# Two PSUM banks for the projections of the local pairs, a bank of its own for their second value batch, another order on GpSimd, and the first local K projected a pair ahead

## The reference, cut to what matters

```python
def even_mixer(h, w_in, w_out, rpb):
    B, T, _ = h.shape
    proj = (h @ w_in).astype(jnp.float32)
    cuts = np.cumsum([W_A, W_A, W_A, W_B, W_B])
    qa, ka, va, qb, kb, vb = jnp.split(proj, cuts, axis=-1)
    ...
    ya = dilated_mixture_attention(heads(qa), heads(ka), heads(va))
    yb = neighborhood_attention(heads(qb), heads(kb), heads(vb), rpb)
    y = jnp.concatenate([ya, yb], axis=1).transpose(0, 2, 1, 3).reshape(B, T, W_A + W_B)
    return y.astype(h.dtype) @ w_out
```

## Time and profile before

| | |
|---|---|
| Runs of the kernel | 2565.6, 2570.64, 2570.91 us, median 2570.64 |
| The profiled execution | 2565.84 us, span 2563.9 us |
| TensorE busy | 2510.9 us, 98% of the span |
| VectorE, ScalarE, GpSimd busy | 1755.5, 1156.1, 413.8 us |
| Granted TensorE clock, mean | 0.993 |
| Pair 3 (with the projection of pair 4) | 247.1 to 309.3 us |
| Pairs 4, 5, 6 | 309.3 to 379.1, to 437.2, to 496.1 us |
| Pair 7 and the first items of the output projection | 496.1 to 545.9 us |

### The profile page before, as it was taken

How to read it: one execution, slowest core, us unless ns; L and a number is a source line. 1 busy time by engine, 2 the same in 40 slices (tenths; PEclk the granted TensorE clock), 3 DMA queues, 4 the chain that set the end, 5 groups by cost and what they waited for, 6 DMA issues and landing times.

```text
span 2563.9 us, 34993 instructions
## 1 busy us (share of the span) xinstructions
PE 2510.9 (98%) x12931; PEld 2068.9 (81%) x12931; DVE 1755.5 (68%) x2647; ACT 1156.1 (45%) x2016; POOL 413.8 (16%) x320
## 2 busy tenths in 40 slices
PE   9999989899999999999999999999999999999998
PEld 7888767778888888888888888888888888888887
DVE  6555545565788888765577777777657878877655
ACT  6555534443433333444455555456434333334444
POOL 1000022310133333200010000000001332332001
PEclk9999999999999999999999999999999999999999
DMA  3222134642344444776411111112233444447754
GB/s 128 61 61 73 38 86 104 157 166 103 133 168 160 162 152 158 281 251 203 147 45 49 44 46 49 49 49 79 107 110 117 167 177 156 145 171 257 238 192 146
DMA packets 189171, 332.38 MB, mean 130 GB/s; under 512 B 59728, under 2 KB 67792, under 8 KB 180816
## 3 DMA queue, kind: packets, MB, share of 16 engines
q1 hardware_dynamic: 154208, 320.62, 36.9%
q10 hardware_dynamic: 34800, 9.60, 1.7%
HBM read 238.24 MB, written 91.91 MB: 129 GB/s over the span
## 4 chain that ended last, share of the span: by engine, by line
PE 92%; DVE 2%; issue 2%; ACT 2%; DMA 1%; SPq 1%; POOL 1%; ACTq 0%; POOLq 0%; DVEq 0%
PE PS L2362 20%; PE PS L2280 18%; PE PS L2281 18%; PE PS L2282 18%; PE PS L2523 4%; PE PS L2455 4%; PE PS L2479 3%; PE PS L2471 1%; PE PS L2429 1%; PE PS L2500 1%; PE PS L2376 1%; PE PS L2504 1%; DVE WS L1585 1%; PE PS L2288 0%; PE PS L2419 0%
## 5 line engine op out<-in xcount | busy, mean ns | idle before, releaser
L2362 PE MATMUL PS<-HH,WS 128*128 128x512 f32 x1536 | 519.8, 405 | 24.5 <-DVE FS L1709 14.1
L2362 PEld LDWEIGHTS PS<-HH,WS 128*128 128x128 f32 x1536 | 287.5, 190 | 84.7 <-DVE FS L1709 15.0
L2362 PE MATMUL PS<-HL,WS 128*128 128x512 f32 x768 | 303.3, 395 | 0.0
L2081 DVE TENSOR_TENSOR SPLIT<-RAWI,SPLIT 128x1024 fp32r<-128x1024 f32 x154 | 195.4, 1271 | 149.2 <-ACT SPLIT L1434 148.7
L1434 ACT ACTIVATE SPLIT<-RAWI 128x1024 fp32r<-128x1024 f32 x154 | 162.9, 1060 | 205.3 <-PE PS L2282 155.8
L2280 PE MATMUL PS<-TH,WS 128*128 128x512 f32 x640 | 249.0, 389 | 0.0
L2281 PE MATMUL PS<-TL,WS 128*128 128x512 f32 x640 | 249.0, 389 | 0.0
L2282 PE MATMUL PS<-TH,WS 128*128 128x512 f32 x640 | 249.0, 389 | 0.0
L2280 PE MATMUL PS<-SPLIT 128*128 128x512 f32 x616 | 240.2, 390 | 0.0
L2282 PE MATMUL PS<-SPLIT 128*128 128x512 f32 x616 | 239.7, 389 | 0.0
L2281 PE MATMUL PS<-SPLIT 128*128 128x512 f32 x616 | 239.7, 389 | 0.0
(11 more groups left out here) (274 smaller groups left out, 4967.0 us busy)
## 6 DMA issues: line engine op xcount, KB each, us to landing
WR<-wstrips SPq DMA_DIRECT2D x224, 256.0 KB, 2.7
RAWI<-ab_scratch SPq DMA_DIRECT2D x154, 256.0 KB, 4.0
ab_scratch<-SIL SPq DMA_DIRECT2D x132, 256.0 KB, 2.0
WD<-wdown SPq DMA_DIRECT2D x22, 1024.0 KB, 6.8
wd_scratch<-WD SPq DMA_DIRECT2D x22, 1024.0 KB, 3.9
RAWI<-wd_scratch SPq DMA_DIRECT2D x88, 256.0 KB, 3.2
UR<-wstrips SPq DMA_DIRECT2D x80, 256.0 KB, 3.1
RAWI<-wdown SPq DMA_DIRECT2D x66, 256.0 KB, 3.7
```

Source lines behind the costliest of these rows:

```text
L2081: e.tensor_tensor(SPLIT[m % 6][:, 1], RAWI[:, m % 4], f(SPLIT[m % 6][:, 0]), ALU.subtract).then_inc(S["ilo"], 1)
L2362: last = e.matmul(ps, wt, xt, start=g == 0, stop=g == 23)
```

## The change

It has six parts. (1) Scores of pairs 4 to 6 take banks 0 and 1 in every slot (`score_bank`); `qk(P, n)` waits for the exps of the slot just before, through the same semaphore. Pair 7 keeps its four score banks. (2) Bank 2 is then a second projection bank (`STRIPE_BANK`): parts 3, 5 and 1 of pairs 5 and 6 go there, parts 3 and 5 of pair 7, and part 1 of pair 4; their `fill` waits for the evacuation of the part before the last one. (3) Bank 3 takes the second value batch (`VALUE_BANK`); for pair 7 it is bank 7. (4) On GpSimd, `kq_low` of parts 2 and 3 stands ahead of `merge_start`, and of parts 4 and 5 ahead of `merge_rest`. On SyncE, `raw` of the second strip stands ahead of `merge_second`, and of the third ahead of `merge_store`. (5) The whole part k = 2 of pair 4 is made in pair 2's last slot, and each later part of pair 4 takes two whole slots of pair 3; the evacuations come a slot earlier, the two weight strips are split in slots 0 and 3 in place of 2 and 5, and `lo` of head 1 is put behind the evacuation of the next slot for n = 1, 3, 5 in place of 0, 2, 4. (6) `spread_rstd` in `classical` moves from ahead of the product k = 2 to the middle of it, 12 matmuls later.

```diff
-    FILLS_TURN = [([(1, 2, 16, 20)], [(1, 2, 20, 24)])]
-    FILLS_TURN += [([(1, k, a, a + 6 + u)], [(1, k, a + 6 + u, a + 12)]) for k in (3, 4, 5) for a, u in ((0, 3), (12, 0))]
-    FILLS_TURN += [([(1, 0, 0, 12)], [(1, 0, 12, 24)])]
+    FILLS_TURN = [([(1, k, a, a + 6 + u)], [(1, k, a + 6 + u, a + 12)])
+                  for k in (3, 4, 5, 0) for a, u in ((0, 3), (12, 0))]
...
-            return [parts[0], [(2, 2, 0, 16)]]
+            return [parts[0], [(2, 2, 0, 24)]]
...
-    START_TURN, START_B, MID_B = {1: 2, 3: 3, 5: 4, 7: 5}, {2: 2, 5: 4, 6: 5}, {3: 3, 7: 0}
+    START_TURN, START_B, MID_B = {0: 2, 2: 3, 4: 4, 6: 5}, {2: 2, 5: 4, 6: 5}, {3: 3, 7: 0}
...
-        return n == 4 if P < 3 else P == 3 and n in (0, 2, 4)
+        return n == 4 if P < 3 else P == 3 and n in (1, 3, 5)
...
-        return {**({1: (3, 0, 5)} if late(P) else {}), 2: (4, 1, 6), 5: (5, 0, 8)}
+        if P == 3:
+            return {0: (4, 1, 6), 3: (5, 0, 8)}
+        return {1: (3, 0, 5), 2: (4, 1, 6), 5: (5, 0, 8)}
...
+    def score_bank(P, n, m):
+        return m if 4 <= P < 7 else 2 * (n % 2) + m
+
+    def fill_bank(P, k):
+
+        if P in (5, 6) or P == 7 and k != 1 or P == 4 and k == 1:
+            return STRIPE_BANK if STRIPE_ORDER[k] % 2 else FILL_BANK
+        return FILL_BANK
+
+    def tv_bank(P, b):
+        return PV_BANK if kind_of(P) != "B" or b == 0 else FILL_BANK if P == 7 else VALUE_BANK
...
+    STRIPE_BANK, VALUE_BANK = 2, 3
...
                     merge_first(P - 4)
-                    merge_second(P - 4)
                 raw(w + ahead + 1, layer)
                 if 4 <= P < 7:
+                    merge_second(P - 4)
+                raw(w + ahead + 2, layer)
+                if 4 <= P < 7:
                     merge_store(P - 4)
-                raw(w + ahead + 2, layer)
...
                 if 4 <= P < 7:
+                    for k in range(2, 4):
+                        kq_low(P + 1, k)
                     merge_start(P - 4)
-                    for k in range(2, 4):
+                    for k in range(4, 6):
                         kq_low(P + 1, k)
...
-                e.wait_ge(S["fill_evac"], 6 * P + place_of(P, k))
-            ps = PS[:, FILL_BANK if bank is None else bank, :]
+                other = P in (5, 6) or P == 7 and k != 1 or P == 4 and k == 1
+                e.wait_ge(S["fill_evac"], 6 * P + place_of(P, k) - (1 if other else 0))
+                if P == 4 and k == 1:
+                    e.wait_ge(S["exp_done"], 1 + 16 * P)
+            ps = PS[:, fill_bank(P, k) if bank is None else bank, :]
...
-            if v_before(P) + b:
+            if tv_bank(P, b) == PV_BANK and v_before(P) + b:
                 e.wait_ge(S["vlo_done"], v_before(P) + b)
...
-                e.wait_ge(S["exp_done"], 1 + 2 * (8 * P + n - 1))
+                e.wait_ge(S["exp_done"], 1 + 2 * (8 * P + n - (n > 0 and P == 7)))
+                if P == 7 and n == 1:
+                    e.wait_ge(S["fill_evac"], 6 * P + 4)
+                    e.wait_ge(S["vlo_done"], v_before(P))
...
-                    if k == 2:
-                        spread_rstd(N)
...
                     for h in range(2):
+                        if k == 2 and h == 1:
+                            spread_rstd(N)
```

More of the change, by code:

```diff
@@ L945, in attention @@
                     merge_rest(P - 4)
-                if P % 8 == 7:
-                    continue
-                for k in range(4 if 4 <= P < 7 else 2, 5 if P >= 8 else 6):
-                    kq_low(P + 1, k)
+                if not 4 <= P < 7 and P % 8 < 7:
+                    for k in range(2, 5 if P >= 8 else 6):
+                        kq_low(P + 1, k)
                 if 1 <= P <= 4:
@@ L1124, in exp @@
             if kind == "B":
-                e.activation(e_tile(kind, m, n)[:, 0:128 * nk], PS[:, 2 * (n % 2) + m, 0:128 * nk], ACT.Exp, scale=-1.0,
+                e.activation(e_tile(kind, m, n)[:, 0:128 * nk], PS[:, score_bank(P, n, m), 0:128 * nk], ACT.Exp, scale=-1.0,
                              bias=ST[:, n % 2, m:m + 1], accum_out=LS[:, P % 2, m, n:n + 1]).then_inc(S["exp_done"], 1)
@@ L1152, in vhi @@
             k = v.shape[1]
-            src = PS[:, PV_BANK, 0:128 * k]
+            src = PS[:, tv_bank(P, b), 0:128 * k]
             if kind_of(P) == "C":
@@ L1671, in scaled_half, with evac @@
                                    op1=ALU.mult).then_inc(S["out_ready"], 1)
-        def evac(P, k, bank=FILL_BANK):
+        def evac(P, k, bank=None):
             e.wait_ge(S["fill_done"], 6 * P + place_of(P, k) + 1)
@@ L1677, in evac @@
             c = 512 * half
-            ps = PS[:, bank, :]
+            ps = PS[:, fill_bank(P, k) if bank is None else bank, :]
             r = RSTD[:, c:c + 512]
@@ L1742, in ttr @@
             c = bias_start(kind, n)
-            s = PS[:, 2 * (n % 2) + m, 0:128 * nk] if kind == "B" else banks(S_BANK[m], 2)[:, 0:128 * nk]
+            s = PS[:, score_bank(P, n, m), 0:128 * nk] if kind == "B" else banks(S_BANK[m], 2)[:, 0:128 * nk]
             e.tensor_tensor_reduce(out=s, in0=s, in1=(table if kind == "C" else table[:, m, :])[:, c:c + 128 * nk],
@@ L1935, in attention_diff @@
                 for v in evacuated(P, n):
-                    evac(*v, PV_BANK if v == (8, 0) else FILL_BANK)
+                    evac(*v, PV_BANK if v == (8, 0) else None)
                 for m in range(2):
@@ L2375, in tv @@
             for k, cols in enumerate(v_columns(P, b)):
-                last = e.transpose(PS[:, PV_BANK, 128 * k:128 * k + 128], cols, IDENT[:, :])
+                last = e.transpose(PS[:, tv_bank(P, b), 128 * k:128 * k + 128], cols, IDENT[:, :])
             last.then_inc(S["tv_done"], 1)
@@ L2439, in qk @@
                         r = slice(64 * m, 64 * m + 64)
-                        last = e.matmul(PS[:, 2 * (n % 2) + m, 0:128 * nk], q_tile(P)[r, a, q], KS[r, P % 2, b, k],
+                        last = e.matmul(PS[:, score_bank(P, n, m), 0:128 * nk], q_tile(P)[r, a, q], KS[r, P % 2, b, k],
                                         start=i == 0, stop=i == 2)
```

## The result

The changed kernel takes 2535.11 us (median of four runs, 2531.75 to 2540.13) against 2568.12 us (four runs, 2564.12 to 2570.91) of the kernel before beside it: a ratio of 0.9874, 95% interval 0.985 to 0.9899. The forecast was 2537 us. The profiled execution took 2532.99 us with a span of 2531.0 us, 32.9 us less than before in both.

What follows compares the result with a forecast made beforehand. TensorE was taken as the bound, busy 2510.9 of 2563.9 us. Gains of 25.6 + 5.6 + 0.7 + 1.7 less 0.7, 1.2 and 0.6 made 31.1 us, giving 2534.7, set at 2537 us for run scatter; range 2530 to 2554.

Steps and rivals of the forecast that it cites:

- Evacuation and value waits: Pairs 3 to 6: TensorE's waits for evacuated projection banks and for value batches go, 25.6 us won together.
- The late strip: Pair 4: the weight strip, loaded earlier, still lands slightly after it is wanted; 0.7 us charged, 0 to 2.
- Clock: Half-clock stretches behind three stalls in pairs 3 and 4 go with the stalls, 5.6 us won.
- One pair of score banks: Pairs 4 to 6: 0 lost in 23 slots, 1.2 us lost at pair 4's entry, between 0.4 and 2.
- Slot 4 of pair 3: `pv` of head 1 waits behind the earlier strip split, evacuation and `y_add`; 0.6 us lost, 0 to 3.
- Pair 7: Value wait of 1.55 us and perhaps half clock go, against a later GpSimd merge; 0.7 won, 3 lost to 4 won.
- The collision: Pair 7: the last `merge_start` on GpSimd can meet VectorE's first split, excluding each other in SBUF; about 1 us lost.
- `spread_rstd`: In `classical`, moved 12 matmuls later, it ends two waits for the statistics; all 1.7 us won.
- the late strip: Rival: late strip or merge in pairs 3, 4 and 7 puts half the waits back, 2546 us; chance 0.13.
- the stalls that move: Rival: TensorE meets VectorE at `pv` or the turns instead of the projection, 2551 to 2555 us; chance 0.12.
- slower score banks: Rival: one pair of score banks turns each of 24 slots into a chain, about 2583 us; chance 0.03.
- The last rival: GpSimd's order does nothing, strip still late, pair 4 keeps 5 of 8.23 us: 2542 us, within the forecast's 0.62.

## Why the prediction was right, step by step

The time was right (2535.11 us for 2537), and the sum too: 31.1 us by the steps, 32.9 in the profile. The steps are not all right, and part of the agreement is luck. The sum has 25.5 us of closed gaps and 5.6 of clock. Measured are 24.5 and 8.4. Had pair 7 gone as in the second profile, where TensorE idles for 10.03 us in it and not for 7.17, the closed gaps would be 21.6 us.

**Evacuation and value waits, 25.6 us.** Right. None of those counted is left in pairs 3 to 6. The parts taken out one at a time return 9.4 us of waits for the projections' bank, 3.7 for the values, and 5.17 at the strip, and the medians follow with 10.3, 5.5 and 9.3 us. Added, and not foreseen, are two waits for the strip's split (0.22 and 0.30 us). In pair 7 a wait of this kind did move: the 1.55 us at the second value transposes turned into 1.74 us at `pv`, and from the first transposes to the first `pv` behind them it is 3.88 us for 5.03.

**The late strip, 0.7 us charged.** The place was right and the charge too high. Counted from the first scores behind the entry (309.30 before, 302.52 after) the load went out at 29.3 us where I had 29.7, and it was wanted at 36.4 where I had 36.8. But I let it land 7 us after its issue, at some 270 GB/s beside the merge loads. It landed in 6.2 us, and when ScalarE came to it at 7.1 us it was held by TensorE and no longer by the transfer.

**Clock, 5.6 us.** The half clock went as I wrote, but busy time fell by more. In pair 3 TensorE is busy for 5.5 us less than before, 1.8 of it the moved matmuls, in pair 4 for 3.2 us less with 323 matmuls in either kernel, and in pairs 5 and 6 for 0.9 and 0.6 us less at the same clock of 1.00. With 0.03 us of pair 7 that is the whole 8.4 us. What goes beyond the clock's 5.6, some 2.8 us, falls on 13 stalls fewer in these pairs (19 and 6 of 0.2 us and more), about 0.2 us each. It is an estimate from these figures of what stopping and starting again costs on top of the wait, and was in no term. Pair 4, for which I wrote about 60 us, lasts 56.0 because its length left out the half clock (2.2 us) and these stops (1.0), and had a charge of 0.7 for the strip.

**One pair of score banks.** Right. 0 for 23 slots is shown by the run with this alone, 1.2 us at the entry by the 1.29 us at 302.52. I had not seen that the price exists only because pair 3's stall ahead of it goes: before, the stall hid it. With pair 3's part undone the wait at the entry is gone again.

**Slot 4 of pair 3, 0.6 us.** Too low: 0.97 us (0.63 in the second profile of the same kernel), and 0.44 at the `pv` behind it. The load went out at 272.55 as forecast, but took 3.2 us to land, not 2.6, and ScalarE waited 1.03 us for it, the one such wait over the 1 us that was to show the sum right. The 12 moved matmuls of this step are 8, 1.8 us and not 2.8: k = 2 went from 16 to 24 in pair 2's last slot.

**Pair 7, 0.7 us won.** The 2.1 us of the profile are luck. Idle time fell from 9.25 to 7.17 us there, but in the second profile the pair is 0.9 us longer than before. TensorE's busy time did not move (40.59 and 40.56 us), so the clock that I counted on came to nothing. Half clock stands at two other places:

```profile
478.70:482.10 3.40, 3.40 (x18) 2.58 (x17) 2.22 (x5) 3.35 (x8) 2.26 (x3) 0.50 1.04 374
492.40:499.20 6.80, 6.18 (x24) 4.83 (x23) 4.92 (x12) 4.35 (x11) 2.90 (x2) 0.50 0.64 202
```

The collision that the prediction took from the Trainium skill (SBUF — State Buffer, section Who interferes with whom) is there: 2.05 us for 1.43, with the last merge beside the split. I had priced it at about 1 us; it costs 0.6 to 0.7. Its time was near: 503 and 511.5 to 512 are 7 and some 15.5 us behind 496.06, and the two parts of the last merge began 5.0 and 15.2 us behind 464.65 (469.68 and 479.84).

**`spread_rstd`, 1.7 us won.** This step failed: "nothing there waits" was argued from its consumer alone. TensorE then met the chain at SIL, two stages later, and over 14 profiles waits as long there as it did for RT, 2.2 us for 2.1 with both places counted.

**The rivals.** None came as a whole. Of the late strip there is slot 4 of pair 3, of the stalls that move there are SIL and pair 7's `pv`; slower score banks did not come at all. The last rival, a strip still late, stood ready: the run with SyncE's old order has a stall of 5.17 us for its 5, and 2544.38 us for its 2542. Against the parts that I had weighed one by one stands how they lean on each other. Alone, the banks win 16.7 us, pair 3 4.5 and the orders 2.3, together 23.5. Taken out of the finished kernel, they cost 10.3 (one bank), 5.5, 8.0, 9.3 and 4.2, together 37.3, against a whole of 29 to 33. The medians' scatter of some 3 us each could make up much of that difference; the rows show one case of it, GpSimd's order. Beside the old banks it brings 0.9 us more at the transpose in pair 7 and takes away no wait for a Q part; beside the new ones it saves 3.9 us in pair 4. It was not run alone. What the half clock adds to each of these is not settled: it came in some executions and not in others.

## What to carry to other kernels

Where TensorE waits for its own output to be evacuated, count a free bank as worth the sum of such waits in the timeline, and look at what the second buffer of another tile does before you leave it there: a double buffer of the scores was hiding nothing in 23 of 24 slots. When stalls go, everything else comes due earlier, so that loads and the work of slower engines have to move ahead in the same edit, and an order that takes away no wait by itself can be worth several microseconds beside it. A wait removed from one point of a chain is won only if TensorE, now earlier, doesn't wait at the next point where it meets that chain.

## What the runs showed of the hardware

**Half clock is no fixed price of a stall.** The stall of 2.45 us in pair 3 has half clock behind it in the kernel before, yet in the run with only the scores changed the granted clock stayed at 1.00 through the same stall of 2.45 us and the 2.29 us one; the eleven waits of up to 1.43 us in the run with one bank brought none. At 5.17, 5.32, 6.71, 7.11 and 8.23 us it fell to 0.50 each time, during the stall or right behind it.

**VectorE and GpSimd disturb each other by amounts that differ from one execution to the next.** The same two VectorE instructions at the same place of pair 7, with GpSimd beside the first, in the kernel after and then in its second profile:

```profile
487.37 4.70 POOL L973 TENSOR_TENSOR Y<-Y,YQ 128x1024 f32<-128x1024 f32 x2
491.24 1.91 DVE L1982 TENSOR_TENSOR HL<-YE,HH 128x1024 fp32r<-128x1024 f32 x1
...
494.26 1.28 DVE L1601 TENSOR_TENSOR WS<-WR,WS 128x512 fp32r<-128x512 f32 x2
```

```profile
488.63 4.70 POOL L973 TENSOR_TENSOR Y<-Y,YQ 128x1024 f32<-128x1024 f32 x2
491.15 3.26 DVE L1982 TENSOR_TENSOR HL<-YE,HH 128x1024 fp32r<-128x1024 f32 x1
...
494.85 2.36 POOL L973 TENSOR_TENSOR Y<-Y,YQ 128x1024 f32<-128x1024 f32 x1 [1.52 <-DMA YQ<-l_scratch]
...
495.52 2.84 DVE L1601 TENSOR_TENSOR WS<-WR,WS 128x512 fp32r<-128x512 f32 x2
```

The first VectorE instruction takes 1.22 us elsewhere in these profiles with GpSimd idle. GpSimd's pair ended at 492.07 in the one execution and at 493.33 in the other, 0.83 and 2.18 us after VectorE's instruction had begun, and that took 0.69 and 2.04 us more than 1.22: as if it had waited for the end of GpSimd's each time. VectorE so comes 1.26 us later to the split, and there meets a third multiplication of GpSimd's, which costs it another 1.56 us (2.84 for 1.28). The two executions differ by 2.3 us, and TensorE's stalls behind these instructions are 0.44 and 0.18 us in the one, 1.78 and 1.74 us in the other. That is 2.9 us more at these two places, and pair 7 is 3.05 us longer in the second: all of the difference between these executions arises here.

**A descriptor issue on ScalarE can take 1.8 us.** In the run with only the orders, one issue (L1185, 258.34) held ScalarE for 1.78 us, where the kernel before took 0.44 at that place, and `pv` waited 0.98 us behind it. Why it took so long is not shown.
